# The sample's FoX and stick-breaking scores as products and sums on VectorE, in place of TensorE transposes and score matmuls

## The reference, cut to what matters

```
z = einsum('bthd,bshd->bhts', q, k) * (HEAD_DIM ** -0.5)      # stick-breaking, t = 1
s = einsum('bthd,bshd->bhts', q, k) * (HEAD_DIM ** -0.5) + cum_q - cum_k   # FoX, t = 1
```

## Time and profile before

| | us |
|---|---|
| median of 3 runs | 3268.46 |
| profiled execution | 3271.95 |
| its span | 3270.1 |
| TensorE busy | 3043.3 |
| VectorE busy | 604.7 |
| ScalarE busy | 401.1 |
| POOL busy | 149.5 |

### The profile page before, as it was taken

The page is one execution under the profiler, slowest core; times in us unless marked ns, Lnnn a source line. Parts: engine busy times, 40 slices in busy tenths (PEclk is TensorE's granted clock), DMA queues, the critical chain, the costliest instruction groups (busy, mean ns, idle before and its releaser), DMA issues.

```text
span 3270.1 us, 40693 instructions
## 1 busy us (share of the span) xinstructions
PE 3043.3 (93%) x14318; PEld 2294.3 (70%) x14318; DVE 604.7 (18%) x1254; ACT 401.1 (12%) x924; POOL 149.5 (5%) x236
## 2 busy tenths in 40 slices
PE   6999999888899999999999999998879999999997
PEld 5878743343588878888878785434337887888886
DVE  2112255411011110000021213543110111000002
ACT  1010022212211010000011001222131101000000
POOL 0000011110000000000000001211100000000000
PEclk9999899978899999999999999997899999999998
DMA  5342133224322212212414322330432222222220
GB/s 168 123 91 61 56 97 107 69 78 120 103 78 78 78 52 78 78 62 71 139 42 122 91 59 60 116 104 25 142 107 86 73 73 78 63 68 77 67 76 27
DMA packets 304830, 272.81 MB, mean 83 GB/s; under 512 B 59282, under 2 KB 274498, under 8 KB 304370
## 3 DMA queue, kind: packets, MB, share of 16 engines
q1 hardware_dynamic: 287826, 260.55, 26.4%
q10 hardware_dynamic: 16800, 9.61, 1.1%
HBM read 260.48 MB, written 17.97 MB: 85 GB/s over the span
## 4 chain that ended last, share of the span: by engine, by line
PE 87%; DVE 3%; issue 3%; ACT 2%; SPq 2%; POOL 1%; DMA 1%; ACTq 0%; POOLq 0%; DVEq 0%
PE ps L553 18%; PE ps L554 18%; PE ps L1008 9%; PE ps L653 7%; PE ps L523 6%; PE ps L590 5%; PE ps L591 5%; PE ps L859 3%; PE ps L926 2%; PE ps L738 2%; PE ps L695 2%; PE ps L929 2%; POOL ring L1260 1%; PE ps L850 1%; SPq L408 1%
## 5 line engine op out<-in xcount | busy, mean ns | idle before, releaser
L553 PE MATMUL ps<-hT,ring 128*128 128x260 f32 x2176 | 657.7, 384 | 10.4 <-DVE hT L1303 10.4
L554 PE MATMUL ps<-hT,ring 128*128 128x260 f32 x2176 | 657.0, 384 | 0.0
L553 PEld LDWEIGHTS ps<-hT,ring 128*128 128x128 f32 x2176 | 415.0, 191 | 75.2 <-DVE hT L1303 11.2
L554 PEld LDWEIGHTS ps<-hT,ring 128*128 128x128 f32 x2176 | 415.2, 191 | 64.3
L1008 PE MATMUL ps<-PT,ring 128*128 128x260 f32 x1408 | 309.1, 383 | 1.7 <-DVE PT L1583 1.7
L1008 PEld LDWEIGHTS ps<-PT,ring 128*128 128x128 f32 x1408 | 267.4, 190 | 43.5 <-issue 2.5
L653 PE MATMUL ps<-arena,ring 128*128 128x127 f32 (+1 forms) x1024 | 238.8, 407 | 0.0
L590 PE MATMUL ps<-hT,ring 128*128 128x260 f32 x704 | 215.5, 388 | 12.4 <-DMA ring<-in_w_in 7.3
L653 PEld LDWEIGHTS ps<-arena,ring 128*128 128x128 f32 x1024 | 209.7, 206 | 24.5
L591 PE MATMUL ps<-hT,ring 128*128 128x260 f32 x704 | 214.4, 387 | 0.0
L523 PE MATMUL ps<-cst,units 128*128 128x128 f32 x960 | 152.4, 287 | 17.0 <-DVE arena L1367 11.6
(11 more groups left out here) (245 smaller groups left out, 2398.6 us busy)
## 6 DMA issues: line engine op xcount, KB each, us to landing
ring<-in_w_in SPq DMA_DIRECT2D x20, 2048.0 KB, 8.1
units<-in_cache_fox_kv SPq DMA_DIRECT2D x256, 128.0 KB, 2.2
units<-in_cache_sb_kv SPq DMA_DIRECT2D x256, 128.0 KB, 2.2
ring<-in_w_ffn_gate SPq DMA_DIRECT2D x22, 1024.0 KB, 5.4
ring<-in_w_ffn_up SPq DMA_DIRECT2D x22, 1024.0 KB, 7.9
ring<-in_w_ffn_down SPq DMA_DIRECT2D x16, 1408.0 KB, 6.2
units<-in_cache_nsa_cmp_kv SPq DMA_DIRECT2D x128, 128.0 KB, 2.2
units<-in_cache_nsa_sel_kv SPq DMA_DIRECT2D x256, 64.0 KB, 1.8
```

The source lines that it names most:

```text
L553: mm(ps[:, b, 0:H2], w, a[:, 0:H2], start=k == 0, stop=k == n - 1)
L554: last = mm(ps[:, b + 1, 0:H2], w, a[:, H2:T], start=k == 0, stop=k == n - 1)
```

## The change

The FoX and stick-breaking units are no longer transposed. The sample's queries of both kinds are transposed once to natural layout (`QNAT`, `qnat`: 8 requests x 512). For each request TensorE broadcasts its 512 query values to all 128 partitions with one matmul into bank 6 or 7 (`ask`). For each unit VectorE then multiplies the unit as loaded (128 x 1024) with the query in PSUM, repeated over four pages, and sums over each 64 (`dots`): 32 dots per layer. The stick-breaking results lie in the layout that the transposes made before (`zT`); the FoX results (`fT`) are turned back by eight matmuls with the identity (`fox_t`). The release of a unit's slot is now the multiply. `KT`'s place is shared by `prod`; the dots wait for the last NSA score. In `in_order` the sample's list is now: NSA steps, then four dots per request, then FoX. Also changed, not shown: counts of semaphores, the buffers (`qs` goes, `qnat` comes), four more transposes at the end of the projection, and the tables that call the new parts.

```diff
@@ -70,9 +70,11 @@
 NU = len(UNITS)
 USLOTS = 6
 NKU = UNITS.index(("selv", 0, 0))
-KSTEPS = {"cmp": 2, "selk": 2, "wink": 1, "fxk": 2, "sbk": 2}
+KSTEPS = {"selk": 2, "wink": 1}
+DOTS = [n for n, u in enumerate(UNITS) if u[0] in ("fxk", "sbk")]
+QNAT = (FXQ, FXQ + 1, SBQ, SBQ + 1)
 UT = (4, 5, 6, 7, 8, 9, 12, 13)
-ACT_CHAIN, DVE_CHAIN = 12, 86
+ACT_CHAIN, DVE_CHAIN = 12, 85
 PAIRS = [("nsa", t) for t in range(4)] + [("fox", 0), ("fox", 1)]
 
@@ -80,11 +82,9 @@
 
 
 
-TURNS = [(u, j) for u in UNITS[2 * NS:NKU] for j in range(KSTEPS[u[0]])]
-_fx = TURNS.index((("fxk", 0, 0), 0))
-TURNS[_fx + 16:_fx + 16] = [(("p_win",), 0)]
-TURNS[_fx:_fx] = [(("p_cmp",), 0), (("p_sel",), 0)]
-TURNS += [(("lf",), 0), (("p_fox",), 0), (("p_new",), 0)]
+TURNS = [(u, j) for u in UNITS if u[0] in KSTEPS for j in range(KSTEPS[u[0]])]
+NTURN = len(TURNS)
+TURNS += [(("p_cmp",), 0), (("p_sel",), 0), (("p_win",), 0), (("lf",), 0), (("p_fox",), 0), (("p_new",), 0)]
 TURN_OF = {t: n for n, t in enumerate(TURNS)}
 BEHIND = CHUNKS.index(("mg", 0, 0))
 CMPT = 4 * NS
@@ -95,9 +95,9 @@
 
 
     dec = [("sc", 0), ("sc", 1), ("sc", 2)]
-    last = {u[0]: n for n, (u, j) in enumerate(TURNS) if u[0][0] != "p"}
+    last = {u[0]: n for n, (u, j) in enumerate(TURNS[:NTURN])}
     done = {last["selk"]: 0, last["wink"]: 1}
-    for n in range(len(TURNS) - 2):
+    for n in range(NTURN):
         dec.append(("turn_s", n))
         if n:
             dec.append(("score_s", n - 1))
@@ -105,9 +105,14 @@
                 dec += [("news", done[n - 1]), ("soft", done[n - 1])]
             if n - 3 in done:
                 dec.append(("weigh_s", done[n - 3]))
-    n = len(TURNS) - 2
-    dec += [("score_s", n - 1), ("news", 2), ("soft", 2), ("zs", 0)]
-    val = [("weigh_s", 2), ("zs", 1), ("turn_s", n), ("zs", 2), ("turn_s", n + 1), ("zs", 3)]
+    p_cmp, p_sel, p_win, lf, p_fox, p_new = range(NTURN, len(TURNS))
+    dec += [("score_s", NTURN - 1), ("news", 1), ("soft", 1), ("turn_s", p_cmp), ("turn_s", p_sel)]
+    for b in range(NS):
+        dec += [("ask", b)] + [("dots", i) for i in range(4 * b, 4 * b + 4)]
+        if b < 2:
+            dec += [[("weigh_s", 1)], [("turn_s", p_win)]][b]
+    dec += [("turn_s", lf), ("fox_t",), ("news", 2), ("soft", 2)]
+    val = [("weigh_s", 2), ("zs", 1), ("turn_s", p_fox), ("zs", 2), ("turn_s", p_new), ("zs", 3)]
     val += [("value_s", b, h) for b in range(NS) for h in range(2)]
     parts = [("scores", 0), ("exp", 0), ("weigh", 0)]
     for n, (u, i) in enumerate(ITEMS):
...
@@ -256,7 +261,8 @@
         SF, PTf = ar(2320, 1025), ar(3348, NPG, 32)
         za, zsp, zw = ar(3604, 256), ar(3860, 256), ar(4116, NPG, 32)
         acc = ar(0, 256)
-        ZS = arena[64:96, 0:1024]
+        prod = ar(5396, 4, 256)
+        zT, fT = ar(0, NPG, NS, 4), ar(3348, NPG, NS, 4)
         LFP = ar(4880, 512)[0:NS * NPG]
         KT = ar(5396, 2, 512)
         sg = [vnat[:, :, :, :].rearrange("p a b c -> p (a b c)")[:, i * T:(i + 1) * T] for i in range(2)]
@@ -339,6 +345,8 @@
         for n, u in enumerate(UNITS):
             if n < 2 * NS:
                 unit_read.append(("kt_ps", 8 * (n // 4) + 4 + n % 4 + 1))
+            elif n in DOTS:
+                unit_read.append(("dot_mul", DOTS.index(n) + 1))
             elif n < NKU:
                 unit_read.append(("kt_ps", CMPT + TURN_OF[u, KSTEPS[u[0]] - 1] + 1))
             else:
...
@@ -830,12 +838,9 @@
                     mm(ps[0:NS, 4, 64:128], C("row8", 64), dg[:, 1, :], start=True, stop=True)
                     last = mm(ps[0:NS, 4, 128:160], C("row4", 32), dg[0:32, 2, 0:32], start=True, stop=True)
                 else:
-                    v = s.rearrange("p (j c) -> p j c", c={"selk": 128, "wink": 128}.get(u[0], 256))
+                    v = s.rearrange("p (j c) -> p j c", c=P)
                     for i in range(4):
-                        if u[0] in ("selk", "wink"):
-                            last = tp(bank[:, i * P:(i + 1) * P], v[:, 4 * j + i, :], P)
-                        else:
-                            last = tp(bank[:, i * P:(i + 1) * P], v[:, i, j * P:(j + 1) * P], P)
+                        last = tp(bank[:, i * P:(i + 1) * P], v[:, 4 * j + i, :], P)
                 last.then_inc(sems["kt_ps"], 1)
 
             def score_s(l, n):
@@ -848,16 +853,25 @@
                 kt = KT[:, SCORE_OF[n] % 2, :]
                 if kind == "selk":
                     last = mm(ps[0:64, 6 + j, :], qn[:, b, :], kt, start=b == 0, stop=b == NS - 1)
-                elif kind == "wink":
+                else:
                     if b == 0:
                         pe.wait_ge(sems["s_ev"], at(pe, "s_ev", l, 1))
                     last = mm(ps[0:64, 6, :], qn[:, b, :], kt, start=b == 0, stop=b == NS - 1)
+                last.then_inc(sems["smm"], 1)
+
+            def ask(l, b):
+
+                if b >= 2:
+                    pe.wait_ge(sems["dot_mul"], at(pe, "dot_mul", l, 4 * b - 4))
                 else:
-                    if b == 0 and h == 0 and j == 0 and kind == "fxk":
-                        pe.wait_ge(sems["s_ev"], at(pe, "s_ev", l, 2))
-                    q, r = (qf, slice(0, 32)) if kind == "fxk" else (qs, slice(32, 64))
-                    last = mm(ps[r, 6 + h, :], q[:, j, b, :], kt, start=b == 0 and j == 0, stop=True, skip_group_check=True)
-                last.then_inc(sems["smm"], 1)
+                    pe.wait_ge(sems["s_ev"], at(pe, "s_ev", l, 2))
+                mm(ps[:, 6 + b % 2, :], ident[0:NS, b:b + 1].broadcast_to([NS, P]), qnat[:, :], start=True, stop=True).then_inc(sems["ask_ps"], 1)
+
+            def fox_t(l):
+                pe.wait_ge(sems["dot_sum"], at(pe, "dot_sum", l, len(DOTS)))
+                for j in range(NPG):
+                    mm(ps[0:32, 6 + j // 4, j % 4 * P:(j % 4 + 1) * P], fT[:, j, :, :].rearrange("p b h -> p (b h)"), ident, start=j % 4 == 0, stop=True,
+                       skip_group_check=True)
 
             def news(l, c):
 
@@ -886,13 +900,7 @@
 
             def zs(l, part):
 
-                if part == 1:
-                    pe.wait_ge(sems["s_ev"], at(pe, "s_ev", l, 4))
-                    apart(pe)
-                    for j in range(NPG):
-                        last = nc.tensor.transpose(ps[:, 7, j * 32:(j + 1) * 32], ZS[:, j * P:(j + 1) * P], ident[64:96, 64:96])
-                    last.then_inc(sems["zt_ps"], 1)
-                elif part == 2:
+                if part == 2:
                     pe.wait_ge(sems["z_sp"], at(pe, "z_sp", l, 1))
                     mm(ps[:, 5, 0:256], C("nupper"), zsp[:, :], start=True, stop=True, skip_group_check=True)
                     for k in range(1, NPG):
...
@@ -1181,8 +1190,8 @@
 
             def zs(l, part):
                 if part == 1:
-                    act.wait_ge(sems["zt_ps"], at(act, "zt_ps", l, 1))
-                    link(fn(za, ps[:, 7, 0:256], ACT.Abs))
+                    act.wait_ge(sems["dot_sum"], at(act, "dot_sum", l, len(DOTS)))
+                    link(fn(za, zT[:, :, :, :].rearrange("p j b h -> p (j b h)"), ACT.Abs))
                     link(fn(za, za, ACT.Exp, scale=-1.0))
                     fn(za, za, ACT.Ln, bias=1.0).then_inc(sems["z_abs"], 1)
                 elif part == 3:
...
@@ -1333,7 +1342,9 @@
                 dve.wait_ge(sems["new_ps"], at(dve, "new_ps", l, 1))
                 for n in range(0, len(NAT), 4):
                     w = min(4, len(NAT) - n)
-                    last = v.tensor_copy(natS[0:NS, n:n + w, :].rearrange("p a b -> p (a b)"), ps[0:NS, n // 4, 0:w * P])
+                    v.tensor_copy(natS[0:NS, n:n + w, :].rearrange("p a b -> p (a b)"), ps[0:NS, n // 4, 0:w * P])
+                v.tensor_copy(qnat[:, 0:256], ps[0:NS, 3, 256:512])
+                last = v.tensor_copy(qnat[:, 256:512], ps[0:NS, 4, 0:256])
                 last.then_inc(sems["new_ev"], 1)
                 dve.wait_ge(sems["new_ev"], at(dve, "new_ev", l, 1))
                 for i, t in enumerate(NATV):
@@ -1351,7 +1362,6 @@
                         v.tensor_copy(dst[:, g * 4 + t:g * 4 + t + 72 * 7 + 1:72], PT[r, t, SEQ:T])
                     for f in range(2):
                         c = 2 * f + g
-                        v.tensor_copy(qs[r, f, :, :].rearrange("p b c -> p (b c)")[:, c:c + 36 * 7 + 1:36], PT[r, SBQ + f, SEQ:T])
                         last = v.tensor_copy(qf[r, f, :, :].rearrange("p b c -> p (b c)")[:, c:c + 36 * 7 + 1:36], PT[r, FXQ + f, SEQ:T])
                 last.then_inc(sems["q_ev"], 1)
                 dve.wait_ge(sems["cum_ps"], at(dve, "cum_ps", l, 1))
@@ -1515,17 +1525,31 @@
                 own(v.tensor_scalar(S[0:rows], S[0:rows], s1[0:rows, c + 2:c + 3], None, ALU.mult), "s_p", l, i + 1)
                 v.tensor_scalar(dg[0:rows, i, 0:rows], ident[0:rows, 0:rows], S[0:rows, n:n + 1], None, ALU.mult).then_inc(sems["dg"], 1)
 
+            def dots(l, i):
+
+                kind, b, h = UNITS[DOTS[i]]
```

(42 more changed lines are left out.)

## The result

The changed kernel takes **3310.32 us** (median of 4 runs, 3303.98 to 3318.83) against 3269.08 for the kernel before beside it (4 runs): a ratio of 1.0128, 95% interval 1.0104 to 1.0152, slower by 41 us. The profiled execution, the slowest of the four, took 3318.83 us, span 3316.8, mean granted clock 0.908; that of before 3271.95, 3270.1 and 0.958. A second set of runs of the same code gave 1.0106 (1.0083 to 1.0129).

The account below looks back on a forecast made before the run. TensorE was taken to bound the kernel before. Per layer -3 + 34 + 2 + 0.5 (projection) = +33.5, twice +67 on 3268.5, gave about 3335 us; forecast 3310 to 3365 (chance 0.48), whole range 3262 to 3378.

Parts of the forecast that it names:

- Second stretch: Row-maximum of item 24 to that of item 41, per layer: from 100.45 us to 135.7, taken as +34.
- C: VectorE's copy of the second transposed head in an item; six waits before it, 19.6 us at the lower clock.
- R: An item's row-maximum on VectorE; waits before it after each branch, 14.8 us at the lower clock.
- First stretch: Row-maximum of item 1 to that of item 24, per layer: from 132.3 us to 129, a gain of 3.
- item loop: Cycle of an item's reciprocal, scalings, transposes and copies; limits items 1 to 23 to 121.3 us at full clock.
- W: An item's reciprocal on VectorE; from one to the next 4.6 us was claimed at width 512.
- After item 41: End of the layer: copy and transposes go, FoX turn comes, cumulative matmuls start at lower clock; +2, bounds -2 and +8.
- costs nothing: SP's loading of key units: 3.1 us a unit against 4.2 by VectorE, six slots full at the start.
- faster rival: TensorE's freed time shortens the kernel: 3228, partly so 3250; dots fill waits, items 24 to 41 at 101.3; chance 0.20.
- TensorE's freed time counts: Rival: items 1 to 24 fall to about 107 us, kernel 3228, partly so 3250; chance 0.20.
- The clock stays full: Rival: TensorE keeps full clock throughout, +11 us a layer, kernel 3290; chance 0.17.
- The lower clock reaches everything: Rival: TensorE's lower clock in all parts, +60 us a layer, kernel 3390; chance 0.09.

Follow-up runs that it names:

- r_thin: Changed kernel with dots that multiply and sum only 16 of each 256 columns: 3252.53 us, 0.9938 of the kernel before.
- r_place: Changed kernel with each dot held back until right behind the next reciprocal or row-maximum on VectorE: 3288.35 us, 1.0043 of the kernel before.
- r_place_warm: r_place plus three filler matmuls on TensorE per dot, feeding nothing: 3267.43 us, 0.9994 of the kernel before.
- r_again: The changed kernel run once more without any edit: 3305.00 us, 1.0106 of the kernel before.
- r_thin_one: r_thin with each FoX and stick-breaking key unit loaded by one issue in place of four: 3257.33 us, 0.9950 of the kernel before.
- r_warm: Changed kernel, full dots, plus three filler matmuls on TensorE per dot, feeding nothing: 3295.61 us, 1.0060 of the kernel before.
- r_thin_warm_one: r_thin_one plus three filler matmuls on TensorE per dot, feeding nothing: 3232.73 us, 0.9876 of the kernel before.
- r_thin_warm: r_thin plus three filler matmuls on TensorE per dot, feeding nothing: 3248.12 us, 0.9932 of the kernel before.
- r_spread_warm: Changed kernel with NSA steps in items 1 to 12, one dot an item in 13 to 40, and fillers on TensorE: 3263.45 us, 0.9982 of before.

## Why the prediction was right, and where its terms were off

The forecast (slower, 3310 to 3365) held, but only just: 3310.3 lies 0.3 us inside it and 25 under the 3335 given, and the second set's median of 3305.0 lies outside. That the direction was right rests on the mechanism; that the first set's time fell inside the narrower range is luck.

*Second stretch: +34 predicted, +28.3 measured.* The mechanism stood. VectorE's own work was put at 101.3 and was 97.7 (32 dots at 2.43 us for 2.5 make 2.2 us of it); waits were put at 34.4 in all and were 31.0. By kind, the waits before C were put at 19.6 us in six places and were 14.3 in five, those before R at 14.8 in three and 13.1 in four. r_thin shows that the dots' time makes the loss, r_place that 12.3 us of it are their place (8.4 with what items 41 to 48 lose by the move), r_place_warm that the clock is worth another 6.2 net. The prediction had 12 us for the clock (135.7 against 123.8). No run here has the clock without the fillers' cost, so the 12 are neither confirmed nor refuted.

*First stretch: -3 predicted, -13.8 measured (-12.4 in layer 1).* This is the mis-sized term, 10.8 and 9.4 us in the two layers. It is nearly all of the error, because the 5.7 that the second stretch came out lower and the 5.7 to 7.0 that the part behind item 41 came out higher cancel. The item loop at full clock summed to 121.3 and the stretch took 118.5 at a granted 0.84. I then took 129, between 121 and the 149 of the lower clock. The failed step is that interpolation: it put 7.7 us on top of the full-clock sum for a swinging clock, and the whole stretch stayed 2.8 under that sum. The sum itself was right only as a whole. It gives 60 to 61 us for each half, and items 1 to 12 took 52.2, items 12 to 24 took 66.3. In the second half the lower clock did reach the path: four of its eight score matmul pairs (L859) took 1.97 us instead of 1.07, and that line is the largest of the chain of waits over 449 to 507 us (18.0%). So the agreement of 118.5 with 121.3 is in part luck; how much of the first half's difference is the 0.4 us allowed for each step left (9.6 in all) and how much the item loop's own sum, no run separates. One reading in that sum is too short: W of the next item stands behind C in VectorE's program, and in r_place it starts 0.60 us after C does (563.65, 564.25), so W to W at width 512 is about 5.0 us, not 4.6. Items 13 to 24 took 58.4 us in nearly every run with this order, with TensorE busy 46 of it. They run the same instructions in all these runs, so that shows only how steady they are; that the item loop and not TensorE ends last there follows from TensorE's 21% of idle time and isn't shown by an experiment.

*After item 41: +2 predicted, +7.7 measured in layer 0 (+9.0 in layer 1).* The prediction's reason for the first part does not hold. It had the cumulative matmuls begin at the lower clock; they took the same 7.93 us as before, in both layers:

```profile
635.88 2.58 PE L873 MATMUL ps<-cst,arena 128*32 128x128 f32 x16
...
638.64 7.93 PE L890 MATMUL ps<-cst,LF 128*32 128x128 f32 x24
```

The FoX turn ahead of them (first row) took 2.58 for the 1.8 predicted. Of the +7.7, 2.6 lie up to item 48: 0.9 by the end of the cumulative matmuls and 1.8 behind it, which weren't traced further. The other 5.1 lie beyond, in code that the change does not touch, at a clock of 0.80 in place of 0.84. The prediction had no term for the latter. It also moves from run to run (75.1 at 0.85 and 78.6 at 0.82 in the two layers of r_again), and that would fit the wider spread of the changed kernel's runs (15 us in the first set, where before has 2). Why the clock is lower there wasn't settled.

*Loads: "costs nothing".* True of the changed kernel as far as the trace shows, since no wait on VectorE names a transfer. But the cover was thin: 3.64 us a unit against 128.7/32 = 4.02. The prediction had 3.1. The floor of 102 us lies 0.7 above the 101.3 of its faster rival, so the loads alone would not have ruled that rival out.

*The rivals.* "TensorE's freed time counts" fell: items 1 to 24 took 118.5 us and not 107, and even with hardly a dot left (r_thin) the kernel gains 0.6%. "The clock stays full" fell with 0.54. The granted clock was 0.54 with TensorE busy 57% of the stretch and 0.90 with it busy 84% (r_place_warm).

The Trainium skill (TensorE: Matmul & The Clock Gate, Part 1) has the clock fall after the array was idle and return under sustained work, so a strict reading gives full clock where matmuls never stop for long. The changed kernel's second stretch doesn't test that reading, since TensorE is idle there for up to 5.67 us at a time:

```profile
525.51 0.41 PE L531 MATMUL ps<-cst,ring 128*31 128x128 f32 x1 [5.67 <-POOL ring L1269]
```

Items 24 to 41 of r_thin_one test it better, and they disagree: no pause between matmuls is longer than 2.1 us, TensorE is busy 74%, and the granted clock is 0.56. In 640 to 684 us of the kernel before, the longest pause is 1.4 us at a clock of 0.59.

"The lower clock reaches everything" fell: the first stretch took 118.5 us at 0.84, not 149. It held in part in items 12 to 24 and behind item 48.

## What to carry to other kernels

Work put on an idle engine that runs in program order is free only where that engine would have waited anyway. In this kernel it paid to give each wait of the critical loop one piece that fits its length, directly behind the instruction that starts the wait, never in front of the one that ends it. Before moving work to shorten a stretch, price the next floors of it (the loop's own latency, the loads' issues with the gaps between them, the other engine's program); here they lay at 98 (at the lower clock), 102 and 98 us beside a stretch of 100, so there was little to win. And price the engine that gets emptier at its lower clock, but only for the matmuls that something waits for.

## What the runs showed of the hardware

- A VectorE multiply of 1024 float32 elements a partition with one operand broadcast from PSUM took 1212 ns, about the 1223 that the size alone gives by the earlier trace rows; a reduce to 16 strided results 1220 ns.
- Matmuls that feed nothing, 1.64 us of TensorE a dot, raised the granted clock of items 24 to 41 from between 0.52 and 0.56 to between 0.82 and 0.94. That shortened them by 3.9 and 6.8 us of 129 (r_warm), 6.2 of 116 (r_place_warm) and 5.5 of 98 (r_thin_warm_one), and by nothing in layer 0 where the loads ended last (r_thin_warm) or the dots were spread (r_spread_warm).
- Four page loads of 128 KB each took SP's queue 2.14 us to issue (r_thin_warm) and one load of the same 512 KB 0.37 to 0.40 us (r_thin_one). Where SP was the floor, at 102 us, that shortened the stretch by 3.9 us, and by 9.8 with fillers.
